# Moving eight cache copies from ahead of the projections to behind the attention

## The reference

```python
h = _rmsnorm(x, norm1_g) * (1 + sc1) + sh1
proj = h @ w_in                                  # q, k, v and three parts of a convolution
for g in range(N_DIL_GROUPS):                    # windows 128, 512, 2048
    o, lse, k_keep, v_keep = attend(g, q[:, :, hs], k[:, :, hs], v[:, :, hs], bias_k)
    states += [k_keep, v_keep]
...
x = x + g1 * (jnp.concatenate([attn, conv_out], axis=-1) @ w_o)
h2 = _rmsnorm(x, norm2_g) * (1 + sc2) + sh2
x = x + g2 * _moe(h2, ...)                       # 64 experts, top 8, one shared expert
```

```python
k_ext = jnp.concatenate([k_buf.astype(k_new.dtype), k_new], axis=1)
v_ext = jnp.concatenate([v_buf.astype(v_new.dtype), v_new], axis=1)
return o, lse, k_ext[:, -Wb:], v_ext[:, -Wb:]
```

## Time and profile before

| | |
|---|---|
| median of 3 runs | 1302.62 us (1299.69 to 1302.67) |
| profiled execution | 1304.99 us, its span 1303.1 us |
| busy, share of the span | PE 86%, PEld 42%, DVE 37%, ACT 16%, POOL 20% |
| moved by DMA | 370.99 MB, 285 GB/s over the span |
| ScalarE's queue (q10) | 32.17 MB, 7.1% of the 16 DMA engines |
| SP's queue (q1), GpSimd's queue (q0) | 258.84 MB, 50.8%; 79.49 MB, 22.9% |

### The profile page before, as it was taken

One profiled execution on the slowest core, in us unless ns is written; L12 is line 12 of the kernel. 1 busy time (PEld: TensorE's weight loads), 2 busy tenths in 40 slices (PEclk: granted clock), 3 DMA queues, 4 the chain that ended last, 5 costly groups with the idle time before them and its releaser, 6 DMA issues.

```text
span 1303.1 us, 17147 instructions
## 1 busy us (share of the span) xinstructions
PE 1119.3 (86%) x6061; PEld 551.4 (42%) x6061; DVE 482.7 (37%) x1081; ACT 211.5 (16%) x464; POOL 260.3 (20%) x282
## 2 busy tenths in 40 slices
PE   5899775887999999698999998998989989899880
PEld 1355442444577756554333333333333333333330
DVE  3455576543245644723222221232212222122225
ACT  1421111000133301302111111011111111111110
POOL 1000222210212040001232331222212222222321
PEclk9999888988979999899999999999999989999995
DMA  9874678664767286319799999999999999999946
GB/s 306 272 254 148 219 236 281 185 153 119 218 211 197 76 311 265 117 41 409 267 392 374 388 375 373 381 390 383 364 368 375 380 381 343 374 380 368 385 105 221
DMA packets 103169, 370.99 MB, mean 285 GB/s; under 512 B 13334, under 2 KB 52779, under 8 KB 78000
## 3 DMA queue, kind: packets, MB, share of 16 engines
q1 hardware_dynamic: 69128, 258.84, 50.8%
q0 software_dynamic: 26368, 79.49, 22.9%
q10 hardware_dynamic: 7636, 32.17, 7.1%
HBM read 342.84 MB, written 66.02 MB: 314 GB/s over the span
## 4 chain that ended last, share of the span: by engine, by line
PE 46%; DMA 39%; DVE 6%; SPq 3%; issue 3%; ACT 1%; POOL 0%; DVEq 0%; ACTq 0%; POOLq 0%
DMA mem<-in_w_up_e 29%; PE pb L1501 14%; DMA mem<-in_w_ada 8%; PE pb L1206 7%; PE pb L1360 4%; PE pb L1521 3%; PE pb L1210 2%; PE pb L1438 2%; PE pb L1116 2%; PE pb L1093 2%; PE pb L1338 2%; SPq L580 1%; PE pb L1281 1%; PE pb L1294 1%; SPq L612 1%
## 5 line engine op out<-in xcount | busy, mean ns | idle before, releaser
L1501 PE MATMUL pb<-mem 128*32 128x512 f32 (+2 forms) x1792 | 352.4, 607 | 25.7 <-DMA mem<-in_w_up_e 25.1
L1501 PEld LDWEIGHTS pb<-mem 128*32 128x32 f32 (+2 forms) x1792 | 120.1, 131 | 244.2 <-issue 243.4
L1521 PE MATMUL pb<-mem 128*32 128x512 f32 (+2 forms) x896 | 177.4, 597 | 2.6 <-issue 2.6
L1990 DVE SCALAR_TENSOR_TENSOR mem<-pb,mem 128x256 f32<-128x256 f32 x48 | 32.4, 676 | 320.7 <-ACT mem L1063 253.3
L1093 PE MATMUL pb<-mem 128*128 128x128 f32 (+3 forms) x644 | 96.2, 287 | 59.3 <-ACT mem L1050 26.6
L1206 PE MATMUL pb<-mem 128*128 128x384 f32 x384 | 136.1, 511 | 0.0
L779 POOL DMA_INDIRECT y_d<-mem x48 | 69.7, 1453 | 299.6 <-DVE mem L1996 159.5
L1093 PEld LDWEIGHTS pb<-mem 128*128 128x128 f32 (+3 forms) x644 | 74.1, 148 | 110.9 <-issue 58.7
L1206 PEld LDWEIGHTS pb<-mem 128*128 128x128 f32 x384 | 74.9, 200 | 57.2 <-issue 14.2
L1521 PEld LDWEIGHTS pb<-mem 128*32 128x32 f32 (+2 forms) x896 | 57.0, 129 | 97.8 <-issue 97.8
L774 POOL DMA_INDIRECT mem<-h_d,mem x54 | 61.0, 1130 | 184.9 <-issue 140.7
(11 more groups left out here) (256 smaller groups left out, 1059.5 us busy)
## 6 DMA issues: line engine op xcount, KB each, us to landing
mem<-in_w_gate_e SPq DMA_DIRECT2D x64, 1024.0 KB, 17.5
mem<-in_w_up_e SPq DMA_DIRECT2D x64, 1024.0 KB, 26.1
mem<-in_w_down_e SPq DMA_DIRECT2D x64, 1024.0 KB, 23.2
mem<-in_w_ada SPq DMA_DIRECT2D x24, 1024.0 KB
mem<-in_w_in SPq DMA_DIRECT2D x8, 1536.0 KB
mem<-new_d POOLq DMA_DIRECT2D x16, 512.0 KB, 6.7
out<-in_cache_k_w ACTq DMA_DIRECT2D x8, 1020.0 KB, 7.3
out<-in_cache_v_w ACTq DMA_DIRECT2D x8, 1020.0 KB, 21.3
```

The costliest lines, as they stand in the source:

```text
L1501: mm = eng.matmul(pb[t % 2][lo:hi, :].rearrange("p (q f) -> p q f", q=2), lhsT=xT[t][:, k, lo:hi], rhs=wgu[c][:, :, k, :], start=(k == 0), ...
L1521: mm = eng.matmul(pb[2 + half][lo:hi, :], lhsT=he[t][:, f, lo:hi], rhs=wdn[c][:, f, 512 * half:512 * half + 512], start=(f == 0), stop=(f ...
```

## The change

The constant that says how many copies are issued ahead of the projections goes from 8 to 0. The order of the list stays. So no copy is issued at L873; the two at L930 and the seven at L957 are now the first nine of the list; and all that is left, 17 copies in place of 9, is issued at L1002.

```diff
-FIRST_COPIES = 8
+FIRST_COPIES = 0
 COPY_ROWS = (32, 128, 256)
 COPY_UNITS = (2, 5)
 COPY_STEPS = range(4, 18, 2)
```

## The result

The changed kernel took **1309.7 us** (median of 7 runs, 1303.93 to 1314.69), the kernel before 1302.0 beside it (7 runs, 1299.69 to 1304.44): a ratio of 1.0064, 95% interval 1.0041 to 1.0087. That is slower, and inside the predicted range of 1303 to 1319. Two later measurements of the same kernel gave 1.0043 (1.0020 to 1.0067) and 1.0036 (1.0013 to 1.0060). All three intervals lie above 1, so the loss is clear of noise, and 0.64% is the largest of three sizes. A ratio here is not the quotient of the two medians beside it, which is 1.0059 for the first.

A forecast was written before the change was run, and what follows sets the result against it. The chain was taken to lie mostly on TensorE and DMA, with the second norm on VectorE deciding here. Early part 0, issue 0, late row write +9.4 us on the median 1302.62 gave 1312.0 us; range 1303 to 1319.

The forecast's parts named there:

- The early part at nothing: In 56 to 88 us, removing eight copies and their issues from ScalarE's queue changes the time by 0 us.
- The bounds of 0.9 us either way: TensorE's weight-load wait after 95 us, beside L930's two copies: gain or loss of at most 0.9 us.
- Issue at nothing: ScalarE's queue at L1002: eight more issues at 637 ns, 5.1 us, done by about 478 us, cost nothing.
- rival 3: ScalarE's queue fills at 17 copies and its sequencer stalls, or large copies crawl: 1317 to 1319 us, chance 0.12.
- The end of the copies at 536.1 to 539.2 us: Late list at L1002: the added copies' 23.7 to 26.8 us of engine time all goes behind 512.4 us.
- SP does not pass: Behind 522.34 us, SP's weight load and first row write, 18 packets an engine, need 36 us and land after the large copies.
- 9.4 us late: Second norm's third row group on VectorE waits for the first row write, until 541.2 us instead of 531.8.
- A slow restart at nothing: TensorE, idle 9 us longer during the norm's wait, restarts at a cost between nothing and 1 us, taken as 0.
- the 5 to 14 us that were called likeliest: The norm waits for its write and the kernel's end moves by this much: 1307.5 to 1316.5 us, chance 0.65.
- rival 1: SP's ring behind 522.34 us: writes pass or the tail is short, delay 0 to 0.5 us, 1302 to 1305, chance 0.19.
- rival 2: Weight loads TensorE waits for between 88 and 140 us: early copies held something up; faster by over 0.3% (3.9 us), chance 0.04.

The follow-up runs named there:

- the eight copies left out: Changed kernel without issuing its last eight copies, the value cache of window 1024: ratio 1.0005 (0.9984 to 1.0027) to the kernel before, median 1300.9 us.
- four copies moved: Against the changed kernel, four copies go back ahead of the projections, leaving 13 at L1002: ratio 0.9998 (0.9974 to 1.0021) to the kernel before, 1300.4 us.
- five repeated writes: Kernel before, with VectorE writing the second norm's third row group five times more, copies unchanged: 1311.8 us, ratio 1.0098 (1.0068 to 1.0127).

## Why the prediction was right

By its own steps:

- **The early part at nothing: right.** TensorE's busy time in 56 to 88 us is the same, its wait for the `in_w_ada` weights is 0.5 us against 0.9, and the eight copies left out gain nothing (1.0005). The bounds of 0.9 us either way hold in the chain.
- **Issue at nothing: right in the sum, wrong in its row.** The prediction took eight more issues at 637 ns, done at 478 us. The trace has (ns minimum, median, maximum):

```profile
L1002 ACTq DMA_DIRECT2D out<-in_cache_v_w x13: 598/627/7775, 465.3 to 489.8; - x13
...
506.95 1.06 ACT L1008 ACTIVATE mem<-mem 32x1024 f32<-32x1024 f32 x1 [48.55 <-DVE mem L1804]
```

  Three issues took 7.8, 7.4 and 2.9 us, and the last began at 489.8. That is the stall of rival 3, and its cover of 33 us held: L1008 waits the same 48.55 us for VectorE as in the earlier trace rows.
- **The end of the copies at 536.1 to 539.2 us: at the upper edge.** Counted from the first issue of L1002 (466.6 in the earlier trace rows) that is 69.5 to 72.6 us. Here the first issue is at 462.1, and the last issue of 489.8 with the longest landing of 45.3 us gives 535.1, so 73.0 us at most.
- **SP does not pass: right,** with 2.4 of its packets for a large one against the 1.9 that the sum used. SP's 18 packets on each engine would need some 27 us at that rate, and the copies had 16.5 us left. The Trainium skill ("DMA: Bandwidth & Descriptors", section "Queues, rings and completion order") has an engine drain a packet of about 9 to 17 descriptors from one queue before it switches. If each packet of the trace is one descriptor, which no run here shows, the trace does not agree: 125 of SP's packets went beside 53 large ones.
- **9.4 us late: right in mechanism, small in size.** VectorE waited 11.1, 10.1 and 9.9 us in three profiles. The execution of after was ahead, but the cover was not changed by that: the third group was ready 9.0 us after the write's issue (527.57 against 518.57), and 9.06 in the earlier trace rows. The landing of 20.0 us less 9.0 is the wait; the sum had 18.0 to 18.5 us for the landing. The 1.7 us between 11.1 and 9.4 are these: the copies ended 16.5 us after the write's issue and not 14.9, the write landed 3.5 us behind them and not 3.0, and VectorE began 0.1 us after the landing and not 0.5.
- **A slow restart at nothing: right here, by 0.5 us.** From the third group's start to the shared gate it is 17.42 us against 16.93. TensorE runs at the lower level in 522 to 550 us (0.53 and 0.50), but has little to do in it, and has the full clock from 550 on. The run with four copies moved shows that a low clock can cost 6.6 us there when no wait covers it, after a second fall that neither of these two profiles has ahead of the shared gate.
- **Size at the end.** The sum added the whole wait to the median. By the medians three measurements gave 7.7, 5.3 and 4.8 us for a stage that was 11 to 12 us longer. So the first result came near to the forecast in part by luck: the wait was longer than forecast and the end moved by less, and the two later measurements lie at the low edge of the 5 to 14 us that were called likeliest. The clock is one candidate for the rest: an execution that does not wait may pay for the restart, one that waits pays inside the wait. The run with five repeated writes in the kernel before, at 12.8 us, speaks against it. It is argued, not shown, and where the rest of the delay goes stays open.

The rivals: the writes did not pass (rival 1), nothing was won in the front by itself (rival 2), and the stall came without effect (rival 3).

## What to carry to other kernels

Before a bulk copy is moved into an empty stretch of the DMA engines, look for who issues a small transfer in that stretch and has a buffer waiting for it: the cover to count is that of the small transfer's landing, here 4.0 us, not the room for the copy. If bulk has to go there, its packet size decides what others pay: the same copies with the small-packet ones last cost nothing that the median shows, with the large ones last some 5 to 8 us. A kernel whose executions scatter by several microseconds before the stage in question is compared by the length of that stage, not by its position in two traces.

## What was unexpected in the hardware

An issue on ScalarE's queue can stall, and it is not the number of copies that decides. The nine late copies of the kernel before, eight large and one with small packets, had no issue over 0.82 us. Nine with four large ones first and five small-packet ones behind them stalled the last; with eight copies left out it took 7.4 us, and 6.3 to 8.0 us in the three other kernels with such a list:

```profile
L1002 ACTq DMA_DIRECT2D out<-in_cache_v_w x5: 598/657/7445, 461.2 to 464.2; - x5
```

With 17 copies the fifth small-packet one took 7.8 us, and the two large ones behind it 7.4 and 2.9. With the large ones in the middle the fourth and the fifth small-packet copy took 3.5 and 28.8 us:

```profile
L1003 ACTq DMA_DIRECT2D out<-in_cache_v_w x13: 532/647/28752, 464.4 to 475.4; - x13
```

With the five small-packet ones first (four copies moved) the longest issue was 2.2 us, of the first large one behind them. So the stalls come with the fourth or fifth small-packet copy or right behind it. A small-packet copy has 256 packets, a large one 16; that the queue fills by packets fits this order, and is not shown. The earlier trace rows has a long issue on SP's queue too, so an issue "well under a microsecond" is the usual case and not a bound.

With the large ones in the middle ScalarE's issuing ran to 504.2 us, and its next work began at 505.92: 1.7 us of cover were left, where the prediction counted 33 for the changed kernel.

Two queues with packets of like size shared the engines evenly in 488 to 500 us of the changed kernel, the window of the earlier trace rows; three such queues did not quite in the window of 517 to 530 us above (619, 415 and 432 packets):

```profile
q10 hardware_dynamic: 647, 2.50, 51.0%
q0 software_dynamic: 642, 2.32, 47.5%
```
